# A four-layer network in one kernel: rows, queries, output weights and side inputs moved earlier around three changes of stage, and RWKV's key norms in another form

## The reference

```python
z = jnp.einsum('bsd,df->bsf', hn, w_in)                      # hn = rmsnorm(h), EvenIn
qa, ka, va, ga, qb, kb, vb, gb = jnp.split(z, 8, axis=-1)    # a: retention, b: stick-breaking
...
z = jnp.einsum('bqhd,bkhd->bhqk', q_blk, k).astype(jnp.float32) * scale
log_1mb = jnp.where(mask, jax.nn.log_sigmoid(-z), 0.0)
after = lax.cumsum(log_1mb, axis=3, reverse=True) - log_1mb
w = jnp.where(mask, jnp.exp(jax.nn.log_sigmoid(z) + after), 0.0)
return jnp.einsum('bhqk,bkhd->bqhd', w.astype(v.dtype), v)
...
return jnp.einsum('bsf,fd->bsd', mixed, w_out)               # LayerEnd, with the gate and side input
...
kk = (k * k_k).reshape(B, S, H, N).astype(jnp.float32)       # RWKV, heads of N = 64
kk = kk / jnp.maximum(jnp.linalg.norm(kk, axis=-1, keepdims=True), 1e-12)
k = k * (1.0 + (a - 1.0) * k_a)
```

## Time and profile before

| | |
|---|---|
| three runs | 3601.2, 3606.47, 3607.1 us |
| the profiled execution | 3604.79 us, its span 3603.0 us, mean granted TensorE clock 0.978 |
| PE busy | 3443.2 us, 96% of the span |
| DVE, ACT, POOL busy | 1961.5, 1734.1, 253.0 us |
| EvenIn 0 to 410 | PE busy 389.7 of 410 |
| Stick 420 to 568 | PE busy 131.7 of 148 |
| end of layer 0, 568 to 805 | PE busy 223.8 of 237 |
| Rwkv 1208 to 1758 | PE busy 515.3 of 550 |
| end of layer 1, 1758 to 2000 | PE busy 222.6 of 242 |

### The profile page before, as it was taken

How to read it: one execution, slowest core, us unless ns; L and a number is a source line. 1 busy time by engine, 2 the same in 40 slices (tenths; PEclk the granted TensorE clock), 3 DMA queues, 4 the chain that set the end, 5 groups by cost and what they waited for, 6 DMA issues and landing times. The chain is left out here.

```text
span 3603.0 us, 48003 instructions
## 1 busy us (share of the span) xinstructions
PE 3443.2 (96%) x18610; PEld 2850.1 (79%) x18610; DVE 1961.5 (54%) x3737; ACT 1734.1 (48%) x3346; POOL 253.0 (7%) x194
## 2 busy tenths in 40 slices
PE   7999898999999999999899999999899999999999
PEld 6888746877887777777787788888778888888787
DVE  3144344355334676775434477777864566666562
ACT  3222364265444455554325566566642665665530
POOL 0011130000001122212000000000100000000100
PEclk9999999999999999999899999999999999999999
DMA  4333503112222222221411211111221211111231
GB/s 147 119 130 126 175 1 119 51 53 88 94 97 94 88 60 60 70 59 51 155 53 41 57 36 36 36 31 43 75 94 65 88 35 42 42 42 42 79 103 47
DMA packets 219338, 263.64 MB, mean 73 GB/s; under 512 B 62700, under 2 KB 142948, under 8 KB 218088
## 3 DMA queue, kind: packets, MB, share of 16 engines
q1 hardware_dynamic: 219112, 260.57, 22.4%
HBM read 190.51 MB, written 69.99 MB: 72 GB/s over the span
## 5 line engine op out<-in xcount | busy, mean ns | idle before, releaser
L332 PE MATMUL bank<-wh,XH 128*128 128x512 f32 x1344 | 536.7, 399 | 13.2 <-DVE wl L316 9.5
L332 PE MATMUL bank<-wl,XH 128*128 128x512 f32 x1344 | 528.5, 393 | 0.0
L332 PE MATMUL bank<-wh,XL 128*128 128x512 f32 x1344 | 528.3, 393 | 0.0
L2725 PE MATMUL bank<-XH,wh 128*128 128x512 f32 x1040 | 423.2, 407 | 0.8 <-DVE vv L3157 0.5
L2725 PE MATMUL bank<-XH,wl 128*128 128x512 f32 x1040 | 407.8, 392 | 0.0
L2725 PE MATMUL bank<-XL,wh 128*128 128x512 f32 x1040 | 406.9, 391 | 0.0
L332 PEld LDWEIGHTS bank<-wh,XH 128*128 128x128 f32 x1344 | 256.4, 191 | 66.2 <-issue 10.1
L316 DVE TENSOR_TENSOR wl<-raw,wh 128x1024 fp32r<-128x1024 f32 x128 | 162.3, 1279 | 263.2 <-ACT wh L307 262.2
L332 PEld LDWEIGHTS bank<-wl,XH 128*128 128x128 f32 x1344 | 255.2, 190 | 54.4
L332 PEld LDWEIGHTS bank<-wh,XL 128*128 128x128 f32 x1344 | 256.3, 191 | 50.7
L332 PE MATMUL bank<-XH,wh 128*128 128x512 f32 x704 | 280.7, 399 | 6.8 <-DVE XL L1598 6.1
(11 more groups left out here) (440 smaller groups left out, 6819.0 us busy)
## 6 DMA issues: line engine op xcount, KB each, us to landing
sc_zt<-stage SPq DMA_DIRECT2D x88, 256.0 KB, 2.0
raw<-in_att_w_in SPq DMA_DIRECT2D x33, 512.0 KB, 4.2
raw<-in_even_w_in SPq DMA_DIRECT2D x32, 512.0 KB, 5.1
raw<-in_odd_w_in SPq DMA_DIRECT2D x32, 512.0 KB, 4.6
raw<-in_rec_w_in SPq DMA_DIRECT2D x32, 512.0 KB, 4.0
sc_h<-H SPq DMA_DIRECT2D x24, 512.0 KB, 2.6
sc_z<-stage SPq DMA_DIRECT2D x40, 256.0 KB, 2.0
z<-sc_z SPq DMA_DIRECT2D x8, 1024.0 KB, 5.5
```

What stands on the lines that cost most here:

```text
L332: done = e.matmul(out, lhsT, rhs, start=k == 0 and j == 0, stop=k == NK - 1 and j == 2)
L2725: done = e.matmul(bank[:, :], x[:, k, :], y[:, k, ts], start=k == 0 and j == 0, stop=k == NK - 1 and j == 2)
```

## The change

1. EvenIn: tile 0 is cut in two, its first four k blocks ("begin") ahead of turn 1; rows 1 and 2 are normed singly; turn s stands ahead of tile s-1; SP loads the third weight part between rows 1 and 2.
2. Stick's first loads are issued at tile 60 instead of 62 (w_out's first load at 62 instead of 60), with queries and keys first under one flag, then the four v under flags of their own that only `pe_weigh` waits for. POOL scales the queries instead of DVE. ACT's table is loaded ahead of its wait.
3. The first half of layer 0's `w_out` is split in Stick, at steps 26, 30, 34 and 38 of its order.
4. Layer 0's end takes rows 4 to 7 first in its first half, PE goes on without waiting for Stick's ends, and in both layer ends the sides stand behind the fourth and fifth row taken.
5. Rwkv: two matmuls with a block matrix `heads2` give each head's sum at all of its 64 rows, so floor, log and exp run on 128x512 and 128x1024, the eight transposes go, and the key is multiplied by `tm` in SBUF with one instruction. The rate on ACT waits for that multiply.

The diff, cut:

```diff
...
-    def __init__(self, c, w_out, p, ple_w, gate_w, h, out, next_gain, post_gain=None, mid_gain=None, mixed=None, begun=1):
-        self.begun = begun if mixed is not None else 0
+    def __init__(self, c, w_out, p, ple_w, gate_w, h, out, next_gain, post_gain=None, mid_gain=None, mixed=None, begun=1,
+                 rows=tuple(range(NS))):
+        self.begun, self.rows = begun if mixed is not None else 0, rows
...
-        self.tile, self.aside = c.flag("pe"), 4 if self.begun > 1 else 0
-        self.w = Weights(c, [w_out[:, 0:512], w_out[:, 512:1024], gate_w[:, 0:512], gate_w[:, 512:1024]], self.tile, 7, early=mixed is not None,
+        self.tile, self.aside = c.flag("pe"), 4
+        self.w = Weights(c, [w_out[:, 0:512], w_out[:, 512:1024], gate_w[:, 0:512], gate_w[:, 512:1024]], self.tile, [rows[-1]] + [NS - 1] * 3, early=True,
...
         halves = [(s, half) for half in range(2) for s in range(NS)]
+        outs = [(s, 0) for s in self.rows] + [(s, 1) for s in range(NS)]
...
-        self.mm = Turns(mm, [("w", *r) for r in halves] + [(x, *r) for r in halves for x in "gp"])
+        self.mm = Turns(mm, [("w", *r) for r in outs] + [(x, *r) for r in halves for x in "gp"])
...
                         self.p[512 + 256 * q:768 + 256 * q, :].rearrange("(a p) n -> p a n", p=P)).then_inc(*self.side[1].up(q))
-        if self.mixed is None:
-            self.w.sp(e, 0)
-        if self.aside:
+        if self.begun != 1:
...
             e.dma_start(self.pg[:, :], row_of(self.post_gain).to_broadcast([P, D])).then_inc(*self.pgin.up())
-        for s in range(2 if self.pg is not None else NS):
+        for s in range(2) if self.pg is not None else self.rows:
...
         wait_all(e, before)
-        for s in range(NS):
+        for x, s in enumerate(self.rows):
             self.pe_out(e, s, 0, marks[s])
-            if 0 <= s - self.aside < 2:
-                self.pe_side(e, s - self.aside)
+            if 0 <= x - self.aside < 2:
+                self.pe_side(e, x - self.aside)
...
         wait_all(e, before)
-        if self.mixed is None:
-            self.w.ve(e, 0)
         self.w.ve(e, 1)
-        for s in range(NS):
-            if s < 2:
-                self.ve_side(e, s)
-            elif s in (4, 5):
-                self.ve_ple(e, s - 4)
+        for x, s in enumerate(self.rows):
+            if x == 2 and self.pg is None:
+                for q in range(2):
+                    self.ve_side(e, q)
+            elif x < 2 and self.pg is not None:
+                self.ve_side(e, x)
+            if x in (4, 5):
+                self.ve_ple(e, x - 4)
...
     def plan(self):
-        order = [("sq", 0, 1), ("scale", 0), ("turn", 0), ("w", 0, 0), ("w", 0, 1), ("sq", 1, 3), ("scale", 1), ("w", 0, 2), ("w", 0, 3),
-                 ("turn", 1), ("scale", 2)]
+        order = [("sq", 0, 1), ("scale", 0), ("turn", 0), ("w", 0, 0), ("w", 0, 1), ("sq", 1, 2), ("scale", 1), ("w", 0, 2), ("w", 0, 3),
+                 ("begin", 0), ("turn", 1), ("sq", 2, 3), ("scale", 2)]
...
         for s in range(2, NS):
-            front[s - 2] += [("sq", *g) for g in self.GROUPS[2:] if g[0] == s + 1] + [("turn", s)] + [("scale", s + 1)] * (s < NS - 1)
+            front[s - 1] += [("sq", *g) for g in self.GROUPS if g[0] == s + 1] + [("turn", s)] + [("scale", s + 1)] * (s < NS - 1)
...
                 e.dma_start(self.g[:, :], row_of(self.gain).to_broadcast([P, D])).then_inc(*self.gained.up())
-                for q in range(3):
+                for q in range(2):
                     self.w.load(e, q)
-            if s == 2:
-                self.w.load(e, 3)
+            if 1 <= s <= 2:
+                self.w.load(e, s + 1)
...
                 if n == 60:
+                    self.guest.sp_first(e)
+                if n == 62:
                     following.first(e)
-                if n == 62:
-                    self.guest.sp_first(e)
...
                 self.features.pe(e)
+            elif what == "begin":
+                self.pe_tile(e, n, range(NK // 2))
             elif what == "tile":
-                self.pe_tile(e, n)
+                self.pe_tile(e, n, range(NK) if n else range(NK // 2, NK))
...
             order.append(("kept", (t - 12) // 3, 0, 0))
+        if t in (26, 30, 34, 38):
+            order.append(("split", (t - 26) // 4, 0, 0))
...
             self.sp_head(e, h)
+        e.wait_ge(*self.even_in.ret.gated.at(NS - 1))
+        self.sp_head(e, 3)
+        for h in range(4):
+            e.dma_start(split3(self.v[h][:, :]), self.z[:, 2048 + h * P:2048 + (h + 1) * P].rearrange("(a p) e -> p a e", p=P)) \
+                .then_inc(*self.values[h].up())
...
         e.dma_start(self.q[h][:, :], self.zt[h * P:(h + 1) * P, :]).then_inc(*self.heads[h].up("q"))
-        e.dma_start(self.k[h][:, :], self.zt[512 + h * P:512 + (h + 1) * P, :]).then_inc(*self.heads[h].up("k"))
-        e.dma_start(split3(self.v[h][:, :]), self.z[:, 2048 + h * P:2048 + (h + 1) * P].rearrange("(a p) e -> p a e", p=P)) \
-            .then_inc(*self.heads[h].up())
+        e.dma_start(self.k[h][:, :], self.zt[512 + h * P:512 + (h + 1) * P, :]).then_inc(*self.heads[h].up())
...
     def sp(self, e, before):
-        e.wait_ge(*self.even_in.ret.gated.at(NS - 1))
-        self.sp_head(e, 3)
...
             e.dma_start(self.g[h][:, :], self.zt[1024 + h * P:1024 + (h + 1) * P, :]).then_inc(*self.gates[h].up())
+        for q in range(3, 7):
+            self.then.w.load(e, q)
...
                 e.activation(c.XH[:, 4 + h, qc], self.g[h][:, qc], ACT.Copy).then_inc(*self.high.up(h, half))
+            elif what == "split":
+                if h == 0:
+                    e.wait_ge(*self.kepl.at(3))
+                self.then.w.ac_part(e, 0, h)
...
     def po(self, e, before):
+        for h in range(4):
+            e.wait_ge(*self.heads[h].at())
+            e.tensor_scalar(self.q[h][:, :], self.q[h][:, :], 128.0 ** -0.5, None, ALU.mult).then_inc(*self.scaled.up(h))
...
         wait_all(e, before)
-        for h in range(4):
-            e.wait_ge(*self.heads[h].at())
-            e.tensor_scalar(self.q[h][:, :], self.q[h][:, :], 128.0 ** -0.5, None, ALU.mult).then_inc(*self.scaled.up(h))
...
                 self.ve_kept(e, h)
+            elif what == "split":
+                self.then.w.ve_part(e, 0, h)
...
         elif what == "norm":
-            key = (what, p)
...
                 e.wait_ge(*self.tables.at("heads2"))
-            wait_all(e, self.bank_free(key))
-            for n in range(NS):
-                done = e.matmul(self.bank(*key)[:, 2 * n:2 * n + 2], self.t[:, self.chunk(n)], self.cols2[:, :], start=True, stop=True)
-            done.then_inc(*self.side.up(what, p))
-        elif what == "unit":
-            e.wait_ge(*self.root.at("spread", p))
...
                 wait_all(e, self.bank_free(key))
-                for j in range(4):
-                    done = e.transpose(self.bank(*key)[:, self.chunk(j)], self.t[:, self.chunk(4 * h + j)], self.c.ident[:, :])
-                done.then_inc(*self.side.up(what, p, h))
+                e.matmul(self.bank(*key)[:, :], self.heads2[:, :], self.t[:, HALVES[h]], start=True, stop=True) \
+                    .then_inc(*self.side.up(what, p, h))
...
         elif what == "norm":
-            e.wait_ge(*self.prep.at("floor", p))
-            e.activation(self.nr[:, :], self.nr[:, :], ACT.Ln).then_inc(*self.root.up(p))
+            e.wait_ge(*self.prep.at("floor", p, 1))
+            e.activation(self.t[:, :], self.t[:, :], ACT.Ln).then_inc(*self.root.up("log", p))
         elif what == "spread":
-            e.wait_ge(*self.root.at(p))
-            e.activation(self.t[:, :].rearrange("p (a e) -> p a e", e=64), last_axis(self.nr[:, :], [P, 2 * NS, 64]), ACT.Exp, scale=-0.5) \
-                .then_inc(*self.root.up("spread", p))
+            e.wait_ge(*self.root.at("log", p))
+            e.activation(self.t[:, :], self.t[:, :], ACT.Exp, scale=-0.5).then_inc(*self.root.up("spread", p))
         elif what == "unit":
-            e.wait_ge(*self.side.at("unit", p, 1))
+            e.wait_ge(*self.prep.at("unit", p))
...
         elif what == "norm":
-            e.wait_ge(*self.side.at(what, p))
-            if p:
-                e.wait_ge(*self.root.at("spread", p - 1))
-            e.tensor_scalar(self.nr[:, :], self.bank(what, p)[:, 0:2 * NS], 1e-24, None, ALU.max).then_inc(*self.prep.up("floor", p))
+            for h in range(2):
+                e.wait_ge(*self.side.at(what, p, h))
+                e.tensor_scalar(self.t[:, HALVES[h]], self.bank(what, p, h)[:, :], 1e-24, None, ALU.max).then_inc(*self.prep.up("floor", p, h))
...
         elif what == "unit":
-            for h in range(2):
-                e.wait_ge(*self.side.at("unit", p, h))
-                if h == 0:
-                    e.wait_ge(*self.scaled.at("kk", p))
```

(8 more changed lines are left out.)

53 lines of the change are left out of this document (30 added, 23 removed).

## The result

The changed kernel takes 3584.35 us (median of five runs, 3581.73 to 3595.74), the kernel before 3607.1 (3601.2 to 3614.54). The ratio is 0.9946, with a 95% interval of 0.9926 to 0.9967: faster by some 19 to 23 us. The forecast was 3569, a gain of 36 to 38. The result lies at the upper end of the range, a little outside, and where rival C put it.

The account below looks back on a forecast made before the run. PE, busy 3443.2 of 3603.0 us, was taken as the bound. Six parts summed to -36.2, giving 3568.6 from the profiled run and 3570.3 from the median; forecast 3569, range 3557 to 3584 at some 0.85.

Parts of the forecast that it names:

- rival C: Rwkv: norms cost more, floor, log and clock together +3 per pair, +18 in six instead of +2; 3585, chance 0.08.
- Parts 1, 2, 3, 4 and 5: EvenIn's front -6.5; Stick's start -11.6; four weight splits in Stick +1.5; end of layer 0 -12.6; end of layer 1 -9.
- Part 3: Four weight splits inside Stick, on ACT and DVE: +1.5 us, between 0 and +4.
- part 2: Start of Stick: earlier loads and POOL's scaling bring the first sum from 434.1 to 422.5, -11.6 us, bounds -14 and -9.
- E: Rival: the clock gives more back at the three stage changes, upper bounds and no norm cost; 3555, chance 0.06.
- Part 6: RWKV's key norms, eight pairs: +2 us in all, bounds -6 and +9.
- the 3.4 that I named as the sign: Rwkv, pairs 2 to 7: PE's wait for the state would be 3.4 us instead of 2.26.
- I take +0.6 for each of six pairs: Rwkv's norms in pairs 2 to 7: floor paid in full, +1.15, transposes only partly saved; 3.6 us in all.
- The bound of +1.5 a pair: Rwkv's norms: upper bound of +1.5 us in each of six pairs, giving +9.
- pairs longer by over 1.5: Rwkv: pair length growing by over 1.5 us, instead of 0.6, would show the forecast wrong.
- -0.8 for the first two: Rwkv's norms in the first two pairs, whose steps have no solve: -0.8 us each, 1.6 in all.
- D: Rival: slower than before, half clock behind the state wait costing 6.4 us in each of six pairs; 3607 to 3615, chance 0.03.

Follow-up runs that it names:

- the first trace: The profiled execution of the changed kernel's first set of five runs: 3595.74 us, the slowest of the five.
- the old norms: The changed kernel with RWKV's key norms put back as before, all moves kept: 3568.63 us, ratio 0.9879 to the kernel before; later set 3566.27.
- the second trace: The changed kernel unchanged, run again in a later set: 3587.34 us, ratio 0.9937 to the kernel before; the traced execution took 3587.20.
- the exponentials behind the last tile: The changed kernel with pair 1's three ACT exponentials moved behind the copy of OddIn's last tile: 3583.99 us, ratio 0.9933 to the kernel before.
- the log from the banks: The changed kernel without DVE's floor, ACT taking the log straight from two banks with a 1e-24 bias: 3573.63 us; later set 3572.12.

## Why the prediction was wrong, point by point

**Parts 1, 2, 3, 4 and 5 were right**, to 0.3 us each, as the table shows. Row 2 was next at the start, EvenIn's own last tile next in Stick, nothing next at the layer ends. Part 3's +1.5 was met partly by luck. One wait among the short blocks grew to 2.86 from 1.63, and the one behind it shrank to 1.03 from 2.08; from the first sum to that first wait both kernels take 97.5 to 97.6 us. The 1.4 comes behind it, where the clock is half for 10.2 us instead of 3.4:

```profile
513.70 0.77 PE L1382 MATMUL bank<-w,v 128*128 128x128 f32 x2 [2.86 <-DVE w L1480]
```

Within part 2 two things were off, with no effect on the time. The clock is not half around the first sum "in either kernel": before, it is for 17.1 us from 423.0; after, it is full there in the first trace and half for 6.8 us from 415.7 in the second. And POOL's scale took 2.77 us, above the 2.4 I had as a bound; twice DVE's 0.69, from which I took it, is only 1.4.

```profile
L1443 POOL TENSOR_SCALAR q<-q x4: 2770/2774/2777, 398.4 to 407.0; 128x1024 f32<-128x1024 f32 x4
```

The four ended by 409.8, and were wanted at 413.8.

One sum of the rivals is off too: E's upper bounds add up to 45.9, which gives 3559 to 3561 and not 3555.

**Part 6 failed, the sum for the pairs.** Its own terms held: the floor is two of 0.68, and delays the state by 1.11 (forecast 1.15), though PE's wait for the state is 2.57 and not the 3.4 that I named as the sign, because PE idles 0.72 earlier in the step already, for ACT's copy of R; the product and the multiply cost what was said (columns: count, duration ns min/median/max):

```profile
L2529 DVE TENSOR_TENSOR kk<-kk,tm x8: 1207/1217/1219, 1099.1 to 1607.7; 128x1024 f32<-128x1024 f32 x8
...
L2181 PE MATMUL bank<-tm,heads x32: 592/592/1192, 1088.8 to 1594.8; 128*128 128x512 f32 x32
...
L2513 DVE TENSOR_SCALAR tm<-bank x16: 671/681/693, 1091.8 to 1597.6; 128x512 f32<-128x512 f32 x16
```

The step that failed is "I take +0.6 for each of six pairs": it sets saved transposes of PE against a delay of the state, and puts the clock behind that delay at nothing. Neither held. Of the transposes only 1.0 us in five pairs came back (28.6 to 27.6 in the table above), because without them PE waits for T's transfer instead; and behind the longer idle time came half clock, 6.8 to 10.2 us a pair where the old norms have none to 6.8. Over pairs 1 to 5, between the old and the new norms in one set, the floor's steps cost 5.5 us and the steps behind them 6.5, the second larger than the first and missing from the sum. So the term was mis-sized: 2.4 a pair in these five, 12.1 in all, and 1.1 in pair 0, instead of 0.6 in each of six. The bound of +1.5 a pair was too low too, and the sign that the forecast gave for being wrong, pairs longer by over 1.5, came true.

**And "-0.8 for the first two" failed**, the pairs whose norms come before any solve. I had counted PE's work alone there. With less of it PE was ready for Rwkv's first T product some 5 us sooner, and the wait for the last tile (5.65 instead of 1.32) left 0.6 of that, or 0.95 in the second trace, where I had 1.6; what I hadn't traced is ACT's queue in the last two tiles, where the log of 1.06 and the exponentials stand ahead of the copy. Behind the longer wait, at half clock, the way from the first T product to the first state product took 8.4 instead of 6.0. Added up between the old norms and the second trace: 2.5 there, 1.1 in pair 0, 12.1 in pairs 1 to 5, nothing in pairs 6 and 7, and 2.4 behind Rwkv's last part, against 18.1 between the two spans. Behind Rwkv the two kernels are the same, and the slower trace has 13.6 us of half clock up to 2000 where the other has 6.8; whether that is the norms' doing no run shows.

**The rivals.** C had the right time (3585) and the right mechanism, the wait for the state and half clock behind it. The time was partly luck: six pairs cost 13 and not 18, and the rest came at the start of Rwkv and behind it, where C had nothing. I gave it 0.08, although the rows that speak for it were before me: the wait for the state was PE's longest repeated wait, and the floor stood in it. D didn't come near: it needed 6.4 a pair.

**The unit's multiply.** It took 1.207 to 1.219 in all eight pairs, so the contention of two SBUF operands with GpSimd that the Trainium skill tells of ("SBUF — State Buffer", "Who interferes with whom") didn't reach it: POOL had nothing at that moment, as argued. Elsewhere the traces agree with that rule. Where POOL has begun a multiply 0.3 to 0.6 us before DVE's multiply of `a` by `lw` (L2539, L2531 in the earlier trace rows), that takes 3.38 instead of 1.21: in two pairs of eight before (not once, as I wrote), and in five after. The next two state products of PE take 6.3 us in pairs of either kind, so this cost nothing.

```profile
L2539 DVE TENSOR_TENSOR bet<-a,lw x8: 1212/3375/3384, 1106.1 to 1616.1; 128x1024 f32<-128x1024 f32 x8
```

## What to carry to other kernels

Price an instruction on the engine that a wait names not by its own length but by what follows that wait, the clock after the longer idle time above all. Price work taken off PE by what PE needs next: if that is a transfer from the same chain, the saving turns into a wait. Here a floor of 1.1 us cost 2.4 a pair, and taking the log straight from the banks gave 13.7 us, some 3 of them at the last tile before Rwkv. Taking eight transposes off PE gave 0.2 a pair. Where two chains end close to each other, filling PE's idle time raised its clock and moved the wait.

## What the hardware did that I had not expected

In some executions a half-clock stretch lasts 24 to 31 us where others have 3 to 14 at the same place, always behind a pair's state that PE waited over 2 us for. Four traces have five such stretches: the changed kernel's first, 23.9 at 1677; the exponentials behind the last tile, 30.7 at 1388 and 27.3 at 1681; the log from the banks, 30.7 at 1590 and, in the later set, at 1381. Each of the four is one of its kernel's two slowest executions in its set; the other ten traces have none there. **One of them**, of the kernel with the log from the banks, at a clock of 0.51:

```profile
1381.00:1412.00 31.00, 29.00 (x147) 24.92 (x147) 13.03 (x14) 11.42 (x27) 13.53 (x9) 0.51 0.21 48
```

PE is busy for 29.0 of its 31 us, so it isn't idle time within that keeps the clock low. In one trace of that kernel (30.7 at 1590) the two steps there took 12.22 and 11.49 us where its other pairs have 8.5 to 11.3 and 6.32, so 6 to 9 us more in all; its five runs lie between 3568 and 3582. What starts such a stretch stays open.
